# A blocked triangular inverse in the delta rule: 16-token diagonal blocks by substitution on VectorE in place of three doubling levels on TensorE

## The reference, cut to what matters

```python
m = where(strict, einsum("bhnid,bhnjd->bhnij", k_beta, k) * decay, 0.0)
a_mat = eye(CHUNK) + m                          # unit lower triangular, one per head and chunk
u = triangular_solve(a_mat, v_beta, left_side=True, lower=True)
w = triangular_solve(a_mat, k_beta * exp(g)[..., None], left_side=True, lower=True)
```

## Time and profile before

| | |
|---|---|
| median of three runs | 1276.56 us |
| profiled run | 1275.36 us, span 1273.6 us |
| TensorE matmuls, busy | 98%, 9782 instructions |
| VectorE, ScalarE, POOL busy | 57%, 56%, 69% |
| DMA | 217.76 MB, mean 171 GB/s |
| mean granted TensorE clock | 0.998 |

### The profile page before, as it was taken

The page is one execution under the profiler, slowest core; times in us unless marked ns, Lnnn a source line. Parts: engine busy times, 40 slices in busy tenths (PEclk is TensorE's granted clock), DMA queues, the critical chain, the costliest instruction groups (busy, mean ns, idle before and its releaser), DMA issues.

```text
span 1273.6 us, 27624 instructions
## 1 busy us (share of the span) xinstructions
PE 1253.4 (98%) x9782; PEld 1169.0 (92%) x9782; DVE 726.5 (57%) x1682; ACT 714.1 (56%) x1294; POOL 878.5 (69%) x386
## 2 busy tenths in 40 slices
PE   9999999999999999999999999999999999999997
PEld 3678899999998898899999999999999999999986
DVE  3989961142487775278565256555533766555633
ACT  3656644453666665477342347666755546666743
POOL 0457957578869888945333237888788877888795
PEclk9999999999999999999999999999999999999999
DMA  9985254345545555733222114555565554555562
GB/s 369 402 344 198 83 198 162 121 159 186 183 149 200 195 176 174 220 106 129 84 68 71 64 66 175 175 180 181 154 182 194 175 180 159 189 182 177 157 196 76
DMA packets 65881, 217.76 MB, mean 171 GB/s; under 512 B 9752, under 2 KB 17176, under 8 KB 62464
## 3 DMA queue, kind: packets, MB, share of 16 engines
q1 hardware_dynamic: 65792, 216.52, 49.7%
HBM read 215.45 MB, written 1.05 MB: 170 GB/s over the span
## 4 chain that ended last, share of the span: by engine, by line
issue 38%; POOL 37%; PE 21%; ACT 1%; POOLq 1%; DVE 1%; ACTq 0%; DVEq 0%
POOL w_lo L630 37%; PE bank L738 10%; PE bank L1071 5%; PE bank L830 3%; PE bank L839 1%; PE bank L834 1%; POOL w_lo L637 1%; POOLq L627 0%; ACT h L1658 0%; POOLq L629 0%; ACT w_hi L1658 0%; PE bank L676 0%; PE bank L884 0%; PE bank L681 0%; PE bank L677 0%
## 5 line engine op out<-in xcount | busy, mean ns | idle before, releaser
L630 POOL TENSOR_TENSOR w_lo<-w_raw,w_hi 128x1024 fp32r<-128x1024 f32 x340 | 814.4, 2407 | 357.1 <-ACT w_hi L1658 355.7
L1658 ACT ACTIVATE w_hi<-w_raw 128x1024 fp32r<-128x1024 f32 (+1 forms) x372 | 377.8, 1020 | 122.0 <-PE bank L839 40.2
L738 PE MATMUL bank<-a_hi,w_hi 128*128 128x264 f32 (+3 forms) x704 | 200.5, 285 | 0.1
L738 PE MATMUL bank<-a_hi,w_lo 128*128 128x264 f32 (+3 forms) x704 | 200.2, 284 | 0.0
L738 PE MATMUL bank<-a_lo,w_hi 128*128 128x264 f32 (+3 forms) x704 | 200.0, 284 | 0.0
L715 PE MATMUL bank<-a_parts,w_hi 128*128 128x256 f32 x960 | 173.8, 284 | 0.2
L715 PEld LDWEIGHTS bank<-a_parts,w_hi 128*128 128x128 f32 x960 | 149.7, 192 | 1.0 <-ACTq L1915 0.5
L715 PE MATMUL bank<-a_parts,w_lo 128*128 128x256 f32 x480 | 135.8, 283 | 0.0
L738 PEld LDWEIGHTS bank<-a_hi,w_hi 128*128 128x128 f32 x704 | 132.9, 189 | 0.4 <-DVE a_lo L3566 0.3
L738 PEld LDWEIGHTS bank<-a_lo,w_hi 128*128 128x128 f32 x704 | 132.9, 189 | 0.1
L738 PEld LDWEIGHTS bank<-a_hi,w_lo 128*128 128x128 f32 x704 | 132.9, 189 | 0.0
(11 more groups left out here) (523 smaller groups left out, 2857.4 us busy)
## 6 DMA issues: line engine op xcount, KB each, us to landing
w_raw<-in_s SPq DMA_DIRECT2D x284, 512.0 KB, 3.7
w_raw<-in_down SPq DMA_DIRECT2D x48, 512.0 KB, 3.5
adaw<-in_w_ada SPq DMA_DIRECT2D x16, 1024.0 KB, 10.9
w_raw<-in_down SPq DMA_DIRECT2D x24, 384.0 KB, 3.1
adab<-in_w_ada_first SPq DMA_DIRECT2D x8, 1024.0 KB, 8.8
ctxt<-in_ctx SPq DMA_DIRECT2D x1, 1024.0 KB, 11.3
x<-in_x SPq DMA_DIRECT2D x1, 1024.0 KB, 15.3
out_h<-h SPq DMA_DIRECT2D x4, 256.0 KB, 2.7
```

What stands on the lines that cost most here:

```text
L630: pool.tensor_tensor(w_lo[:, s], w_raw[:, s], w_hi[:, s].bitcast(F32), ALU.subtract) \
L738: ins = mm(banks[bank][:, tk], w_[:, s, k], x_[:, k, tk], start=(m == 0), stop=(m == 3 * KD - 1))
L1658: return nc.scalar.activation(out_, in_, f, **kw)
```

## The change

For chunks 1 and 2 the diagonal blocks of 16 tokens (8 blocks x 8 heads x 2 chunks = 128 matrices) are inverted at once on VectorE, one matrix in each partition, by substitution. The levels 1 to 3 of these chunks, `fI1`, `fI2`, their two prefills and predicated copies are gone; chunk 0 is as before, and levels 4 to 6 of chunks 1 and 2 stay.

ScalarE copies the 32 x 32 diagonal blocks of `mt` (all 16 heads of the two chunks, four copies by groups of 32 partitions) into `compact`. VectorE transposes them in 32 x 32 blocks to `lanes_in`, one pair of blocks for each partition, picks the partition's own block with two selector columns `lane` (made by two reductions of the identity), and eliminates for j = 1 to 14. Two transposes bring the inverse and its transpose back, and ScalarE copies them into `tt` and `uu`, which VectorE has cleared earlier. The order of TensorE's stages is written anew:

```diff
-        for c in (1, 2):
-            o_ = arena + 17408 + 12288 * (c - 1)
-            B = {n: at(f"{n}{c}", [P, HN, P], o_ + 4096 * i) for i, n in enumerate(("mt", "tt", "uu"))}
+        chunks12 = {n: at(f"{n}12", [P, 2 * HN, P], arena + 17408 + 8192 * i) for i, n in enumerate(("uu", "tt", "mt"))}
+        lanes_in = at("lanes_in", [P, GB, 2, GB], arena + 41984)
+        compact = [at(f"compact{i}", [P, 2 * HN, 32], area_a + 17536 + 2048 * i) for i in range(2)]
 # TensorE: y(c, lv), ty(c, lv)
+                if c and lv == 4:
+                    pe.wait_ge(mt_ready, 2 * c)
+                    pe.wait_ge(uu_filled, TT_READY)          # ty: UU_READY
 # TensorE's order
             products("kk2", 2, kr)
-            a_in(11, 12) ... flip("fI1"), a_in(12, 13) ... flip("fI2"), y(1, 1), y(2, 1)
+            a_in(11, 13)
             products("kk0", 0, kr)
-            a_in(13, 14), ty(1, 1), ty(2, 1), a_in_part(14, 0, 3), turned(1, 1), turned(2, 1), a_in_part(14, 3, KD)
+            a_in(13, 15)
             pe.wait_ge(mt_scaled, 5)
             flip("fI0", 0, "uu")
-            y(1, 2), y(2, 2)
             y(0, 1)
             a_in(15, 16)
             ty(0, 1)
-            ty(1, 2), ty(2, 2), a_in_part(16, 0, 3), turned(1, 2), turned(2, 2), a_in_part(16, 3, KD)
+            a_in(16, 17)
             turned(0, 1)
-            y(1, 3), y(2, 3)
             pe.wait_ge(ksq_ready, 2 * HN)
             head_rows("hq", ksq, 0, N2, N2)
             y(0, 2)
             a_in(17, 18)
             ty(0, 2)
-            ty(1, 3), ty(2, 3), a_in_part(18, 0, 3), turned(1, 3), turned(2, 3), a_in_part(18, 3, KD)
+            a_in(18, 19)
             turned(0, 2)
             products("kq1", 1, qr), products("kq2", 2, qr)
 # ScalarE
+            def blocks_from(i, name):
+                act.wait_ge(blocks_ready, i + 1)
+                for rows_ in groups:
+                    ins = fn(chunks12[name][rows_, :, rows_], compact[i][rows_], ACT.Copy)
+                ins.then_inc(uu_filled, 1)
-            prefill(1) ... prefill(2)
             tap3(11), rounded(11)
-            flipped("fI1", 1, "tt")
             product_out(2, 3)
-            flipped("fI2", 2, "tt")
+            for rows_ in groups:
+                ins = fn(compact[0][rows_], chunks12["mt"][rows_, :, rows_], ACT.Copy)
+            ins.then_inc(uu_filled, 1)
             activated(10), squared(10), tap3(12), rounded(12), activated(11), squared(11)
             tap3(13), rounded(13), activated(12), squared(12), product_out(0, 5)
-            flipped("f1.1", 1, "uu"), flipped("f2.1", 2, "uu")     # so for f1.2, f2.2, f1.3, f2.3
             tap3(14), rounded(14), activated(13), squared(13), flipped("fI0", 0, "tt")
...
             tap3(17), rounded(17)
+            blocks_from(0, "tt")
             activated(16), tap3(18), rounded(18), activated(17), flipped("f0.2", 0, "uu")
+            blocks_from(1, "uu")
 # VectorE
+            low = banks[6][:, 0:GB * GB].rearrange("p (i j) -> p i j", i=GB)
+            def blocks_to_lanes():
+                dve.wait_ge(uu_filled, MT_COPIED)
+                link(v.transpose(lanes_in.rearrange("p i b j -> p (i b j)"),
+                                 compact[0].rearrange("p g (s i) -> p i g s", s=2)))
+            def own_blocks():
+                link(v.tensor_scalar(low, lanes_in[:, :, 0], lane[:, 0:1], None, ALU.mult))
+                link(v.scalar_tensor_tensor(low, lanes_in[:, :, 1], lane[:, 1:2], low, ALU.mult, ALU.add))
+                link(v.tensor_copy(tri[:], low))
+                link(v.memset(tri.rearrange("p i j -> p (i j)")[:, 0::GB + 1], 1.0))
+            def eliminated(j0, j1):
+                for j in range(j0, j1):
+                    n = GB - 1 - j
+                    part = banks[6][:, GB * GB:GB * GB + n * j].rearrange("p (i c) -> p i c", i=n)
+                    link(v.tensor_tensor(part, low[:, j + 1:, j:j + 1].broadcast_to([P, n, j]),
+                                         tri[:, j:j + 1, 0:j].broadcast_to([P, n, j]), ALU.mult))
+                    link(v.tensor_tensor(tri[:, j + 1:, 0:j], tri[:, j + 1:, 0:j], part, ALU.add))
+            def blocks_apart():
+                for s in range(2):
+                    ins = v.tensor_scalar(lanes_in[:, :, s], tri[:], lane[:, s:s + 1], None, ALU.mult)
+            def lanes_to_blocks(i, view):
+                v.transpose(compact[i].rearrange("p g (s c) -> p c g s", s=2), lanes_in.rearrange(view)).then_inc(blocks_ready, 1)
             differences(0)
+            v.memset(chunks12["tt"][:], 0.0)
             taps(7, 8)
+            v.memset(chunks12["uu"][:], 0.0)
...
-            key_products(1, 1, 2), key_products(2, 2, 3), flipped("fI1"), taps(10), flipped("fI2"), taps(11, 12)
-            masked(1, 1), masked(2, 1), key_products(0, 3, 4), taps(13), added, flipped ... (levels 1 to 3 alike)
+            key_products(1, 1, 0), key_products(2, 2, 0)       # 0: no predicated copy
+            taps(10, 11)
+            blocks_to_lanes(), own_blocks()
+            taps(12)
+            key_products(0, 3, 2)
+            eliminated(1, 4), taps(13), eliminated(4, 7), taps(14)
+            masked(0, 1), eliminated(7, 10), taps(15), added(0, 1)
+            eliminated(10, GB - 1), blocks_apart()
+            lanes_to_blocks(0, "p i b c -> p c b i"), lanes_to_blocks(1, "p i b c -> p i b c")
+            taps(16)
             dve.wait_ge(stage_done, DONE["hq"])
             masked(0, 2), taps(17), added(0, 2), taps(18)
```

More of the change, by code:

```diff
@@ L36 @@
 GRID = 64
+GB = 16
 HN = 8
@@ L271, in bass_two_blocks @@
         hb = tiny("hb", [HN, 4])
+        lane = tiny("lane", [P, 2])
         wba = tiny("wba", [P, KD, 40])
@@ L437, in bass_two_blocks @@
         STAGES = [("masks", (4, 7)), ("ba", (5, 6)), ("rows", (7,)), ("g1", (4, 5)), ("g2", (6, 7)), ("g0", (4,)), ("hk", (6,)),
[L438 to L443, removed]
[3 rows of a table added]
+        EXTRA = {4: ([("y0.3", (7,)), ("ckq", (5,))], [("ty0.3", (7,))],
                      [("f0.3", (7,)), ("kt1", (4, 5)), ("kt2", (6, 7))]),
@@ L464, in bass_two_blocks @@
         QUARTERS = (slice(0, GC), slice(GC, P))
+        groups = [slice(32 * q, 32 * q + 32) for q in range(P // 32)]
         def firsts(ap, lv):
@@ L1337, in ty @@
                 read_out(f"y{c}.{lv}")
-                if lv > 1:
+                if c and lv == 4:
+                    pe.wait_ge(uu_filled, UU_READY)
+                elif lv > 1:
                     read_out(f"f{c}.{lv - 1}")
@@ L3125, in key_products @@
                                                      ALU.mult, ALU.mult)
-                    link(ins)
-                    for i in range(n):
-                        ins = v.copy_predicated(B["uu"][0:cn, heads.start + i], pairs_mask[0:cn, 0:cn], src[:, i])
+                    if filled:
+                        link(ins)
+                        for i in range(n):
+                            ins = v.copy_predicated(B["uu"][0:cn, heads.start + i], pairs_mask[0:cn, 0:cn], src[:, i])
                     ins.then_inc(mt_scaled, 1)
@@ L3245, in _ @@
             differences(2)
+            for s in range(2):
+                v.tensor_reduce(lane[:, s:s + 1], ident[:, s::2], mybir.AxisListType.X, ALU.add)
             taps(6)
             differences(0)
+            v.memset(chunks12["tt"][:], 0.0)
             taps(7, 8)
+            v.memset(chunks12["uu"][:], 0.0)
             ss = banks[6][0:HN, 0:N2]
@@ L3267, in _ @@
             dve.sem_inc(taken[7], 1)
[L3268 to L3277, removed]
+            key_products(1, 1, 0)
+            key_products(2, 2, 0)
+            taps(10, 11)
+            blocks_to_lanes()
+            own_blocks()
+            taps(12)
+            key_products(0, 3, 2)
+            eliminated(1, 4)
             taps(13)
[L3279 to L3282, removed]
+            eliminated(4, 7)
             taps(14)
-            masked(1, 2)
-            masked(2, 2)
             masked(0, 1)
+            eliminated(7, 10)
             taps(15)
             added(0, 1)
[L3290 to L3293, removed]
+            eliminated(10, GB - 1)
+            blocks_apart()
+            lanes_to_blocks(0, "p i b c -> p c b i")
+            lanes_to_blocks(1, "p i b c -> p i b c")
+            taps(16)
             dve.wait_ge(stage_done, DONE["hq"])
             v.tensor_scalar(tok[:, 9], banks[5][0:HN, 0:N2], 1e-6, P * 1e-6, ALU.add, ALU.mult).then_inc(taken[5], 1)
-            taps(16)
-            masked(1, 3)
-            masked(2, 3)
             masked(0, 2)
@@ L3302, in _ @@
             added(0, 2)
[L3303 to L3306, removed]
             taps(18)
```

58 lines of the change are left out of this document (14 added, 44 removed), and 3 rows, old and new, of the table STAGES.

## The result

| | median, us | lowest to highest | profiled run (span) | mean clock |
|---|---|---|---|---|
| before, run beside it | 1276.14 | 1275.07 to 1277.78 | 1275.36 (1273.6) | |
| after | 1266.13 | 1264.83 to 1266.64 | 1264.83 (1263.0) | 0.996 |

The ratio is 0.9921 [0.991, 0.9933]: 10.0 us faster, where 14.1 were forecast. 1266.13 lies in the stated range (1259 to 1268), but beyond the forecast's own range (1260 to 1264.5).

The account below looks back on a forecast made before the run. TensorE's queue was taken as the bound: 20.2 us removed less 6.1 of waits gives 14.1 gained, so 1261.3 profiled and 1262.5 median. Own range 1260 to 1264.5 (54%), stated range 1259 to 1268.

Parts of the forecast that it names:

- the walk: Queues set beside each other with their waits: y1.4 starts at 638.8, not 652.9, 14.1 us gained, profiled run 1261.3.
- the 20.2 us that leave the queue: TensorE up to y1.4: removed products and transposes, old waits and tile restarts sum to 20.2 us less.
- First wait: TensorE before fI0 stands 0.8 us, 606.3 to 607.1, for VectorE's chain of block transpose, own blocks, taps and key products.
- Second wait: TensorE before y0.1 stands 3.5 us for ScalarE's tt, behind activated(13) and squared(13); y0.1 starts at 611.0.
- third wait: TensorE before hq stands 1.7 us for squared(15), with only f0.1 left to cover it; hq starts at 620.4.
- A granted clock of 1.00 at 611 to 618: Sign to look for: TensorE keeps its full 2.4 GHz after the wait before y0.1; a drop there makes the forecast wrong.
- Rival 1: TensorE's clock falls to 1.2 GHz in the wait before y0.1, slowing tile 15: 3 to 4 us back, 1265.9; 19%.
- Small steps 0.2: VectorE's elimination: 28 linked operations of 14 to 56 elements at 0.2 us each, 5.5 us in all.
- Rival 4: Slower than before: VectorE's elimination chain replaces TensorE's queue; losing the whole gain needs each small step at 0.7 us; 4%.
- Slack of the lane work: On VectorE the lane work ends at about 621.0, 3.8 us before taps(16) is free at 624.8.
- The memsets: Two VectorE memsets of 2048 elements near 578 and 584 us, at most 2.7 us each, counted as no loss.
- The stretch behind `y1.4`: From y1.4 on, queues, banks and weights are as before; its length changes by no more than 1 us.

Follow-up runs that it names:

- cover_more: cover_all plus chunk 0's key products ahead of the lane transpose and eliminations from j = 7 behind masked(0, 1): 1255.87 us, ratio 0.9845 to the kernel before.
- forms: Changed kernel with the first transpose reading and writing adjacent elements and blocks_apart reading from PSUM; blocks land in wrong places: 1265.76 us, one run.
- no_lanes: Changed kernel without ScalarE's block copies and VectorE's lane work, so inverses of chunks 1 and 2 are missing: 1262.53 us, ratio 0.9891 to the kernel before.
- clock_kept: Changed kernel with dummy matmuls on TensorE, 16 ahead of the wait before fI0 and 28 before y0.1: 1266.54 us, ratio 0.9931 to the kernel before.
- tile15_first: Changed kernel with tile 15 on TensorE ahead of y0.1 and tile 16 between y0.1 and ty0.1: 1259.42 us, ratio 0.9876 to the kernel before.
- clock_kept_b: Changed kernel with 8 dummy matmuls on TensorE ahead of the wait before fI0 and 14 before y0.1: 1263.23 us, ratio 0.9898 to the kernel before.
- kp0_early: Changed kernel with chunk 0's key products moved ahead of the transpose into lanes on VectorE: 1263.22 us, ratio 0.9904 to the kernel before.
- twice: cover_more with the product of each elimination step issued twice, 14 more linked VectorE operations: 1256.60 us, ratio 0.985 to the kernel before.
- cover_all: Changed kernel with tiles and stages reordered on TensorE and VectorE to cover each of the three waits, nothing left out: 1256.22 us, ratio 0.9851 to the kernel before.

## Why the prediction was right, and what in it was wrong

The stated range held. The forecast's own case, at 54%, did not: a rival's mechanism, the clock, came on top of waits that were right in place and nearly right in size. By the prediction's own steps, with the profiled run's 1264.83 against the 1261.3 of the walk:

- **What bounds it, and the 20.2 us that leave the queue: right.** In after 59.62 - 48.30 = 11.3 us are gained; with the three waits (2.00 + 3.62 + 1.64 = 7.3) and the 1.6 that tile 15 took too long that is 20.2. cover_more, which has no wait, gives 20.3 directly. "256 matmuls fewer" was a miscount in the list of signs; the sum was made with all four groups, which are 448.
- **First wait, forecast 0.8: 2.0.** The term was mis-sized by 1.2: four block copies 2.56 and not 2.1, the transpose 1.09 and not 0.7, the rest in small parts of `own_blocks` and the start. The copies are a size between two rows and lay inside their bounds (0.64 each, 0.25 to 1.05). For the transpose the hop was in the view's shape, and forms shows that it is the cause. The rule named there, from the Trainium skill, Vector Engine (DVE) Microarchitecture Reference, 5.2, gave 1.0 to 1.4, and this case's traces agree: 1.09, and 1.00 each for the two that go back.
- **Second wait, 3.5: 3.6. Third, 1.7: 1.6.** Right, place and releaser too. Between `fI0` and `y0.1` nothing of TensorE's stands. From `activated(13)` at 611.93 to `y0.1` are 1.19 us, before 1.18, where 64 products covered it; what the elimination ahead of `taps(13)` adds is 1.4 of the 3.6 (no_lanes).
- **The clock: the step that failed.** "A granted clock of 1.00 at 611 to 618" was 0.50 up to about 617.2. That is one of the signs by which the prediction called itself wrong. Rival 1, at 19%, came about, with its price of 3 to 4 us too high for the fall it spoke of: 1.6 (after against clock_kept: 1.5). The argument against it, that eight transposes break the wait up, was wrong twice over: 0.35 us of work between waits of 2.0 and 3.6 did not keep the clock, and a wait of 2.0 (tile15_first) or 2.3 (no_lanes) alone was enough to lose it. That rival 1's 1265.9 lies beside the median of 1266.13 is luck: it had neither the longer first wait nor the second fall, and its price was twice too high.
- **The third wait and the clock: not seen.** It can start a fall of its own. In after's profiled run it did not, but it did in clock_kept_b, kp0_early, no_lanes and forms. A run with both falls takes some 2 us more behind `y0.1` (31.0 to 31.9 in kp0_early, no_lanes and forms, against 29.4). The mean clock of after's other runs is 0.993 to 0.994 against 0.996 in the profiled one, and they took 1.3 to 1.8 us longer, which fits a second fall. So does forms, whose order on TensorE is that of after: with both falls in its trace, a mean clock of 0.994 and a first wait 0.4 shorter it took 1265.76. As the three runs of after have no trace, their second fall is argued and not shown.
- **The rule of the page.** The Trainium skill, TensorE: Matmul & The Clock Gate, Part 1, holds that an idle TensorE loses its clock and must work to get it back. The traces agree in that each fall in this stretch stands in or behind a wait of 1.6 us or more and ends while TensorE works; but the waits of 1.6 in after and clock_kept had no fall behind them.
- **Small steps 0.2: nearly right**, 0.16 to 0.23 each, linked, and 0.20 to 0.26 from start to start, so that the 28 took 6.5 us and not 5.5. Rival 4 needed 0.7 and is dead; twice shows it by time, too.
- **Slack of the lane work, 3.8 us: 0.8.** It ended at 627.92, `taps(16)` could start at 628.71. Of the 3.0 lost, 1.9 are `blocks_apart` (2.76, forecast 0.9) and 0.6 the transposes back (1.99, forecast 1.4). It cost nothing here:

```profile
628.71 1.56 DVE L3072 SCALAR_TENSOR_TENSOR vr<-bank,pv,vr 128x269 f32<-128x269 f32 x3 [0.79 <-ACT vr L1641]
```

- **The memsets, counted as nothing: right.** They took 1.76 us each, under the bound of 2.7, and tile 11 started at 592.85 to 593.88 in the nine experiments, which have them, and at 593.30 before.
- **The stretch behind `y1.4`: right**, 620.5 us against 620.7.

Sum of the profiled run, measured less forecast: 1.2 (first wait) + 0.1 (second) - 0.1 (third) + 1.6 (clock) - 0.2 (behind) = 2.6 of the 3.5 missed. The other 0.9 arose before any changed instruction of TensorE: tile 11 started at 594.21 and in the nine experiments, whose code up to there is the same, at 592.85 to 593.88, so that it is taken for variation between runs. The median of 1266.13 is 4.8 above the walk's 1261.3 (the forecast of the median had 1.2 of that): it holds the same 2.6 and, with 1.6 to 2.5 us, the likely second fall.

How much of the waits is whose was open in the prediction: no_lanes gives 3.9 us to the order and 3.4 to the lane work. The removed products had two uses: the work itself and the cover for chunk 0's chain. The 10 us that a plain reading of the removed work would have added are all to be had by moving tiles: cover_all and cover_more have them.

## What to carry to other kernels

When work is taken out of a full queue, list what it was covering: here each level's 64 products stood between two dependent steps of a short chain. Without them TensorE stood for 7.3 us, 3.9 of it by the order of the stages alone and 3.4 by the new lane work, and moving tiles and stages into the gaps brought all of it back. A wait of TensorE also puts its clock at risk, and that comes as slow matmuls behind the wait: read the granted clock in windows around every new wait and price it beside the wait. For small instructions on VectorE count the chain by instructions (here 0.20 to 0.26 us from start to start at 14 to 56 elements), and look at two things for the larger ones: whether the view hops, and what POOL does at that moment.

## What the runs showed of the hardware that was not expected

- A multiplication by a scalar column, 256 elements per partition from SBUF to SBUF, took 2.5 us when it started with a POOL instruction and 0.30 when POOL was idle (cover_more). VectorE and POOL in after (start, length):

```profile
623.13 0.35 DVE L3215 TENSOR_SCALAR lanes_in<-tri,lane 128x256 f32<-128x256 f32 x1
...
623.40 2.50 DVE L3215 TENSOR_SCALAR lanes_in<-tri,lane 128x256 f32<-128x256 f32 x1
```

```profile
620.05 2.39 POOL L635 TENSOR_TENSOR w_lo<-w_raw,w_hi 128x1024 fp32r<-128x1024 f32 x1 [6.68 <-ACT w_hi L1641]
623.40 2.35 POOL L635 TENSOR_TENSOR w_lo<-w_raw,w_hi 128x1024 fp32r<-128x1024 f32 x1 [0.96 <-ACT w_hi L1641]
```

The first multiplication ended as POOL's `w_lo` began; the second lasted until 625.90, just past `w_lo`'s end at 625.75. Read from PSUM (forms) each took 0.44 beside the same `w_lo`. The Trainium skill, SBUF — State Buffer, Terms, says that the two engines contend for one pair of ports, held for a whole instruction, with the loser blocked; these numbers agree.
- The clock was at 1.2 GHz for 3.4 us in some falls and 6.8 in others (3.4 in tile15_first and in both falls of no_lanes, 6.8 in after). It could begin after TensorE had gone back to work: in tile15_first the wait ended at 608.46, and the clock fell at about 610.2. The wait of 1.6 us before `hq` had a fall behind it in clock_kept_b, kp0_early, no_lanes and forms, and none in after and clock_kept: what tells these apart is open.
- The fillers, products of the identity, 128 x 128, took 0.23 us each from start to start in clock_kept, as two matmul instructions in the trace: 28 of them lasted 6.45 us, so they are coarse.
